# A fourth dense tile by accumulating DMAs, and the last tile's lists made inside the expert sweep

## What is computed

```python
def peer(h, w_pq, sub_keys, u_tab, v_tab):
    q = (hf @ w_pq).reshape(T, PEER_HEADS, 2, PEER_HALF)          # 8 heads, 2 halves of 128
    s = jnp.einsum('thsd,hskd->thsk', q, sub_keys)                # 128 sub-keys per half
    s_top, i_top = lax.top_k(s, PEER_TOPK)                        # 16 best per half: "lists"
    cand_s = (s_top[:, :, 0, :, None] + s_top[:, :, 1, None, :])  # 16 x 16 candidates
    f_s, f_pos = lax.top_k(cand_s, PEER_TOPK)                     # 16 pairs per head
    ids = jnp.take_along_axis(cand_i, f_pos, axis=-1)             # "decode": 128 ids per token
    g = jax.nn.softmax(f_s)
    u = jnp.take(u_tab, eb, axis=0)
    a = jax.nn.gelu(jnp.einsum('tkd,td->tk', u, xb), approximate=False)
    return jnp.einsum('tk,tkd->td', wb * a, jnp.take(v_tab, eb, axis=0))
```

## Time and profile before

| | us |
|---|---|
| median of 3 runs | 3486.44 (3481.64 to 3489.65) |
| the profiled execution | 3488.68 |
| its span, first to last instruction | 3486.9 |
| of it: inputs of the mixer | about 340 |
| middle stage, to its end at | 1168.2 |
| one-hot stage (weigh), to its end at | 1318.7 |
| two sweeps and what follows | the rest |
| PE busy | 3315.8 (95%) |
| DVE busy | 2639.6 (76%) |
| POOL busy | 1314.3 (38%) |
| ACT busy | 1274.5 (37%) |

### The profile page before, as it was taken

The page is one execution under the profiler, slowest core; times in us unless marked ns, Lnnn a source line. Parts: engine busy times, 40 slices in busy tenths (PEclk is TensorE's granted clock), DMA queues, the critical chain, the costliest instruction groups (busy, mean ns, idle before and its releaser), DMA issues.

```text
span 3486.9 us, 46941 instructions
## 1 busy us (share of the span) xinstructions
PE 3315.8 (95%) x17312; PEld 2792.9 (80%) x17312; DVE 2639.6 (76%) x5361; ACT 1274.5 (37%) x2402; POOL 1314.3 (38%) x824
## 2 busy tenths in 40 slices
PE   8999999999998477999999999999999999999997
PEld 3656367787887467999999999998999999999996
DVE  0223127888888996888888888889899998888866
ACT  1232133343332593333333333333434333333333
POOL 1000000788886005777775232322233333232201
PEclk9999999999998898999999999999999999999998
DMA  9300544666666149999999999998998999999943
GB/s 397 137 20 8 229 163 164 196 169 180 178 178 190 73 193 349 353 353 348 347 346 364 354 358 355 375 354 332 368 356 347 373 363 354 360 349 360 352 163 124
DMA packets 270605, 952.87 MB, mean 273 GB/s; under 512 B 74281, under 2 KB 127657, under 8 KB 211121
## 3 DMA queue, kind: packets, MB, share of 16 engines
q1 hardware_dynamic: 154898, 521.75, 40.4%
q0 software_dynamic: 115200, 428.07, 34.6%
q10 hardware_dynamic: 288, 0.16, 0.0%
HBM read 888.70 MB, written 61.18 MB: 272 GB/s over the span
## 4 chain that ended last, share of the span: by engine, by line
PE 60%; DVE 1%; DMA 0%; ACT 0%; issue 0%; SPq 0%; DVEq 0%; ACTq 0%
PE bank L1561 30%; PE bank L1575 30%; DMA uw<-in_u 0%; DVE slots L1692 0%; DMA vw<-x_scratch 0%; DVE uL L1756 0%; DVE ring L1668 0%; DVE st L1716 0%; DVE slots L1713 0%; DVE slots L1731 0%; DVE hL L1660 0%; DVE slots L1734 0%; DVE vL L1751 0%; ACT hR L1609 0%; DVE accS L1685 0%
## 5 line engine op out<-in xcount | busy, mean ns | idle before, releaser
L1524 POOL DMA_INDIRECT ring<-in_uv,slots x384 | 587.7, 1530 | 1217.4 <-DVE accS L1685 976.1
L143 POOL DMA_INDIRECT g_cells<-slots x384 | 670.7, 1747 | 381.5 <-DVE slots L1217 248.1
L1561 PE MATMUL bank<-hR,uR 128*128 128x384 f32 x2048 | 689.0, 336 | 18.2 <-DVE uL L1756 18.2
L1561 PE MATMUL bank<-hR,uL 128*128 128x384 f32 x2048 | 688.9, 336 | 0.0
L1561 PE MATMUL bank<-hL,uR 128*128 128x384 f32 x2048 | 687.6, 336 | 0.0
L1685 DVE SCALAR_TENSOR_TENSOR accS<-ring,cs,accS 128x1024 f32<-128x1024 f32 x381 | 489.5, 1285 | 13.6
L1575 PE MATMUL bank<-vR,cR 128*128 128x512 f32 x1536 | 477.5, 392 | 0.7 <-DVE slots L1692 0.7
L1575 PE MATMUL bank<-vR,cL 128*128 128x512 f32 x1536 | 476.0, 391 | 0.0
L1575 PE MATMUL bank<-vL,cR 128*128 128x512 f32 x1536 | 475.7, 391 | 0.0
L1622 ACT ACTIVATE cR<-ga 128x384 fp32r<-128x384 f32 x256 | 134.6, 526 | 927.8 <-PE bank L1575 831.2
L1668 DVE CUSTOM_DVE_ANT_0 ring<-ring,slots 128x1024 f32<-128x1024 f32 x384 | 467.0, 1253 | 0.0
(11 more groups left out here) (240 smaller groups left out, 4007.1 us busy)
## 6 DMA issues: line engine op xcount, KB each, us to landing
uw<-in_u SPq DMA_DIRECT2D x256, 512.0 KB, 6.2
vw<-in_v SPq DMA_DIRECT2D x256, 512.0 KB, 7.3
wr<-in_w_pq SPq DMA_DIRECT2D x36, 2048.0 KB
wr<-in_w_o SPq DMA_DIRECT2D x18, 2048.0 KB
g_cells<-free POOLq DMA_DIRECT2D x32, 768.0 KB, 7.1
g_blocks<-stage SPq DMA_DIRECT2D x12, 2048.0 KB, 6.3
gw<-g_blocks SPq DMA_DIRECT2D x32, 768.0 KB, 14.0
gw<-g_cells SPq DMA_DIRECT2D x32, 768.0 KB, 9.6
```

Source lines behind the costliest of these rows:

```text
L143: pool.indirect_dma_start(out=g_dram[1][:, :], out_offset=bass.IndirectOffsetOnAxis(ap=slots[:, i, D + k:D + k + 1].bitcast(U32), axis=0), ...
L1524: pool.indirect_dma_start(out=ring[:, k % R, :], out_offset=None, in_=a["uv"], in_offset=bass.IndirectOffsetOnAxis(ap=ids[:, k // P, k % P ...
L1561: mm = pe.matmul(A[t][:, 0:CW], w[:, t, k, :], h[:, k, :], start=(k == 0 and w is uR and h is hR), stop=(k == DK - 1 and w is uL))
```

## The change

Three things, which need each other.

1. **Tile 3 moves from one-hot to DMAs.** DMA_TILES = (3, 0, 1, 2) get their g by indirect DMAs, so POOL issues 512 of them instead of 384; tile 3's go to g_blocks, whose four blocks for it are stored with zeros before (16 more DMAs in mixer_inputs). Only tiles 4 and 5 (ONE_HOT) are left in weigh. GROUPS is now a list written out; 16 groups run in the middle stage, three in weigh (LATE = 19), and 13 in the sweep, which at two DMAs per step fill its first 104 steps. In decode tile 3's cell numbers take five small operations on DVE (token, cell0). SP waits for tile 3's last group before the first load of gw.
2. **Tile 8's lists and decode leave the middle stage.** Its scores are left in a new tile, carry (which lies outside the stages' own memory and also serves as xt, hT, s, and two of the three accumulators). DVE makes the lists and the decode in sixteen pieces (PIECES) in the sweep's steps 1, 6, ... 76, between uL and ga; ACT makes two spreads and one exponential there. The gathers of tile 8 wait for routed. In the middle stage residual_in of tile 8 moves ahead of the lists of tile 7.
3. **The buffer of v is two deep for the first 84 steps** (VBUF), since the third part of vw holds the pieces' small tiles; from step 84 it is three again.

```diff
 EARLY = 16
+LATE = 19
+DMA_TILES = (3, 0, 1, 2)
+ONE_HOT = (4, 5)
-GROUPS = wavefront()
+GROUPS = list(in_turn((1, 1, 2, 1, 2, 3, 2, 3, 0, 0, 1, 0, 0, 2, 0, 0, 3, 0, 0, 1,
+                       3, 2, 1, 3, 2, 1, 3, 2, 1, 3, 2, 3)))
...
 def place(pool, slots, g_dram, placed, d, h, first=0, last=TOPK):
-    i = DENSE[1][d]
+    i = DMA_TILES[d]
...
+                for b in range(P // TB):
+                    for part in range(4):
+                        pool.wait_ge(zeroed[part], (NZ // 4 + b) * 16)
+                        ks = slice(part * NKEY // 4, (part + 1) * NKEY // 4)
+                        pool.dma_start(g_dram[0][ZB + b, :, ks, :].rearrange("p k t -> p (k t)"),
+                                       zero[:, 0:NKEY // 4 * TB]).then_inc(zeroed[part], 16)
...
-                    if n > 2 * H:
+                    if 0 <= n - 2 * H - 1 < LAST * H:
                         spread(*divmod(n - 2 * H - 1, H))
...
-                spread(NT - 1, H - 1)
-                exps(NT - 1)
...
                     if h == 0 and i >= 3:
                         decode(i - 3)
-                    if 0 <= i - 2 < NT:
+                    if h == 0 and i - 1 == LAST:
+                        residual_in(LAST)
+                    if 0 <= i - 2 < LAST:
                         lists(i - 2, h)
-                    if h == 0 and 0 <= i - 1 < NT:
+                    if h == 0 and 0 <= i - 1 < LAST:
                         residual_in(i - 1)
-                decode(NT - 1)
...
-        DT = DENSE[0]
+        DT = ONE_HOT
...
                 pool.iota(iob[:, :], pattern=[[1, P]], base=0, channel_multiplier=0,
                           allow_small_or_imprecise_dtypes=True).then_inc(const, 1)
+                for d, h in GROUPS[EARLY:LATE]:
+                    place(pool, slots, g_dram, placed, d, h)
...
+    VBUF = [g % 2 if g < 84 else g % 3 for g in range(GT)]
+    VUSE = [VBUF[:g].count(VBUF[g]) for g in range(GT)]
+    PIECES = {1 + 5 * x: divmod(x, 3) for x in range(3 * H + 4)}
...
-                    if g >= VB:
-                        sp.wait_ge(v_l, g - VB + 1)
-                    sp.dma_start(vw[:, g % VB, :], a["v"][g % NEt, :, :]).then_inc(v_in[g % VB], 16)
+                    b = VBUF[g]
+                    if VUSE[g]:
+                        sp.wait_ge(v_l, max(x for x in range(g) if VBUF[x] == b) + 1)
+                    elif b == 2:
+                        sp.wait_ge(routed, NT)
+                    sp.dma_start(vw[:, b, :], a["v"][g % NEt, :, :]).then_inc(v_in[b], 16)
...
                         if n == 0:
+                            if m == 0:
+                                sp.wait_ge(placed[0], PAIRS * 16)
                             sp.dma_start(gw[:, b % 2, :].rearrange("p (c w) -> p c w", c=CB),
...
+                    if g in PIECES:
+                        part, piece = PIECES[g]
+                        if part < H:
+                            (best_8, next_8, pairs)[piece](part)
+                        elif part == H:
+                            (compare, select_0, select_1)[piece]()
+                        else:
+                            store()
```

More of the change, by code:

```diff
@@ L55 @@
 DENSE = ((3, 4, 5), (0, 1, 2))
+LAST = NT - 1
 NS = len(STILES)
@@ L61, with in_turn @@
 EARLY = 16
+LATE = 19
 RATE = 2
-def wavefront():
-    place = {(d, h): 4 * d + 2 * h for d in range(CT) for h in range(PH)}
-    return sorted(place, key=lambda dh: (place[dh], dh[0]))
-GROUPS = wavefront()
+DMA_TILES = (3, 0, 1, 2)
+ONE_HOT = (4, 5)
+ZB = DENSE[0].index(DMA_TILES[0]) * P // TB
+def in_turn(order):
+    seen = {d: 0 for d in order}
+    for d in order:
+        yield d, seen[d]
+        seen[d] += 1
+GROUPS = list(in_turn((1, 1, 2, 1, 2, 3, 2, 3, 0, 0, 1, 0, 0, 2, 0, 0, 3, 0, 0, 1,
+                       3, 2, 1, 3, 2, 1, 3, 2, 1, 3, 2, 3)))
 class Count:
@@ L1490, in _ @@
                             if m == 0:
-                                for d in range(CT):
+                                for d in range(1, 1 + CT):
                                     sp.wait_ge(placed[d], PAIRS * 16)
@@ L1523, in gather @@
                         pool.wait_ge(v_done, k - R + 1)
+                    if k == STILES.index(LAST) * P:
+                        pool.wait_ge(routed, NT)
                     pool.indirect_dma_start(
@@ L1642, in _ @@
                         act.activation(ga[:, x % 2, :], A[x % 2][:, 0:CW], ACT.Gelu).then_inc(a_ev, 1)
+                    if g - 1 in PIECES:
+                        part, piece = PIECES[g - 1]
+                        if (part, piece) == (1, 1):
+                            spread(0)
+                        if (part, piece) == (H, 0):
+                            exps()
+                        if (part, piece) == (H, 1):
+                            spread(1)
                     if g in NSTEP:
@@ new lines, in next_8 @@
+                def next_8(g):
+                    sl4 = range(4 * g, 4 * g + 4)
+                    for l in sl4:
+                        ins = dve.max(top[:, l, 8:TOPK], s[:, l, :])
+                    ch.step(ins)
+                    for l in sl4:
+                        ins = dve.max_index(ti[:, l, 8:TOPK], top[:, l, 8:TOPK], s[:, l, :])
+                    ins.then_inc(listed, 1)
+                    dve.wait_ge(listed, H * LAST + g + 1)
+                    dve.tensor_copy(itb[:, 4 * g:4 * g + 4, :], ti[:, 4 * g:4 * g + 4, :]).then_inc(key_in, 1)
+                    pair = top[:, 4 * g:4 * g + 4, :].rearrange("p (h w) k -> p h w k", w=2)
+                    dve.tensor_tensor(
+                        cand[:, :, 0:PAIRS].rearrange("p h (a b) -> p h a b", b=TOPK),
+                        pair[:, :, 0, 0:8].rearrange("p h (a o) -> p h a o", o=1).to_broadcast([P, 2, 8, TOPK]),
+                        pair[:, :, 1, :].rearrange("p h (o b) -> p h o b", o=1).to_broadcast([P, 2, 8, TOPK]),
+                        ALU.add)
+                    ch.step(dve.tensor_tensor(cand[:, :, PAIRS:CAND], pair[:, :, 0, 8:TOPK],
+                                              pair[:, :, 1, 0:1].to_broadcast([P, 2, 8]), ALU.add))
@@ new lines, in pairs @@
+                def pairs(g):
+                    for half in range(2):
+                        sl = slice(half * 8, half * 8 + 8)
+                        for h in range(2):
+                            ins = dve.max(fs[:, 2 * g + h, sl], cand[:, h, :])
+                        ch.step(ins)
+                        for h in range(2):
+                            ins = dve.max_index(fp[:, 2 * g + h, sl], fs[:, 2 * g + h, sl], cand[:, h, :])
+                        ch.step(ins)
+                        if half == 0:
+                            for h in range(2):
+                                ins = dve.match_replace(cand[:, h, :], fs[:, 2 * g + h, sl], cand[:, h, :], LOW)
+                            ch.step(ins)
@@ new lines, in select, with select_0 @@
+                def select(half):
+                    part = eq[:, 8 * half:8 * half + 8, :, :]
+                    dve.wait_ge(key_out, H * LAST + half + 1)
+                    dve.tensor_tensor(part, part, key[:, :, :, :], ALU.mult).then_inc(decoded, 1)
+                    dve.wait_ge(decoded, LAST + half + 1)
+                    for n in (8, 4, 2):
+                        ch.step(dve.tensor_tensor(part[:, :, 0:n, :], part[:, :, 0:n, :], part[:, :, n:2 * n, :], ALU.add))
+                def select_0():
+                    select(0)
@@ new lines, in select_1, with store @@
+                def select_1():
+                    select(1)
+                def store():
+                    for w in range(2):
+                        ins = dve.tensor_tensor(out[:, w, :].rearrange("p (h s) -> p h s", h=PH),
+                                                eqw[:, :, w, 0, :], eqw[:, :, w, 1, :], ALU.add)
+                    ch.step(ins)
+                    dve.scalar_tensor_tensor(slots[:, LAST, D:D + PAIRS].bitcast(U32), out[:, 0, :], float(NKEY),
+                                             out[:, 1, :], ALU.mult, ALU.add)
+                    dve.wait_ge(e_out, NT)
+                    ch.step(dve.tensor_reduce(hm[:, :], fs[:, :, :], axis=AX.X, op=ALU.add))
+                    ch.step(dve.reciprocal(hi[:, :], hm[:, :]))
+                    dve.tensor_tensor(
+                        slots[:, LAST, D + PAIRS:].rearrange("p (h k) -> p h k", h=PH), fs[:, :, :],
+                        hi[:, :].rearrange("p (h o) -> p h o", o=1).to_broadcast([P, PH, TOPK]),
+                        ALU.mult).then_inc(routed, 1)
+                    dve.wait_ge(routed, NT)
```

145 lines of the change are left out of this document (114 added, 31 removed).

## The result

| | before | after | second profile of after |
|---|---|---|---|
| median (lowest to highest) | 3485.61 (3481.64 to 3489.65), 4 runs | 3436.53 (3427.03 to 3444.26), 4 runs | 3436.42 (3428.08 to 3438.68), 5 runs |
| span of the profiled execution | 3486.9 | 3424.9 | 3436.5 |
| POOL's first scatter at | 611.67 | 608.26 | 609.78 |
| from there to the end of the middle stage | 556.7 | 528.4 | 535.3 |
| one-hot stage | 150.5 | 121.5 | 122.0 |

What follows compares the result with a forecast made beforehand. TensorE was taken to bound the sweep, but not the middle stage's end or the one-hot stage. Terms -27 - 29 + 1.5 + 1 = -53.5 us turn the profiled 3488.7 into 3435.2, median 3433; range 3408 to 3458.

Steps and rivals of the forecast that it cites:

- The likeliest case: Whole kernel: the forecast itself, all terms summing to -53.5 us, so 3433; chance 0.56.
- POOL ends the middle stage: Rival, middle stage: landing gaps or scatters meeting decode push POOL's 16 groups past 1141, to 1150; kernel 3442; chance 0.1.
- End of the middle stage, -27: Middle stage without tile 8's lists and decode ends at 1141 instead of 1168.2: 27 us won, bounds 33 and 18.
- 1128, or 1140 with gaps of 5.9: Middle stage: time in us when POOL finishes its 16 groups, with landing gaps of 2.5 or of 5.9.
- The four neighbours' waits: Middle stage: four places where two groups of one tile follow each other on POOL, 2.5 us of landing each.
- still ahead of 1141, just: Middle stage: POOL, done by 1128 or 1140, ends before the stage's new end at 1141.
- The one-hot stage, -29: One-hot stage: one scatter per 2.74 us while DVE works; POOL ends it after about 121.5 us, 29 us won.
- The rival in which a scatter does not wait: Rival, one-hot stage: scatters do not wait for DVE, whose 102.8 us set the stage; kernel 3414; chance 0.15.
- Start of the sweep, +1.5: Start of the sweep: SyncE waits for tile 3's last scatter before loading g's weights; 1.5 us lost, bounds 0 and 6.
- The sweep, +1: Sweep: pieces hidden in DVE's spare time, scatters and two v buffers nearly free; 1 us lost, bounds 0 and 25.
- The rival of a stretched sweep: Rival, sweep: two v buffers, u behind g and 40 more scatter steps cost 25 us; kernel 3458; chance 0.14.
- The zero stores: First stage: 16 more zero stores go out while POOL has nothing else to do; no cost.

Runs made afterwards that it cites:

- second profile of after: The changed kernel as it is, nothing altered, run and profiled once more: 3436.42 us.
- a later run: Changed kernel with scatters reordered in the middle stage, two groups in the one-hot stage, tile 8's residual_in behind tile 7's lists: 3428.26 us.
- the version without the wait: Changed kernel with all three edits, plus three scatters of tile 2 between tile 3's two groups in the one-hot stage: 3401.84 us.
- the first experiment: Changed kernel with two groups instead of three in the one-hot stage, tile 2's group moved to the sweep: 3424.83 us.

## Why the prediction was right

**The time.** 3433 was forecast and 3436.5 measured. The likeliest case came true in the first profile of the changed kernel; in the second the rival "POOL ends the middle stage" did, in a smaller size (535.3 us from the first scatter, where 1150 - 611.7 is 538). That the median lies as close as 3.5 us is in part luck: which engine ends the middle stage, with ends 7 us apart, is decided by about 1 us between a scatter and a load, and the working had nothing of that.

**End of the middle stage, -27.** -28.3 in the first profile, -21.4 in the second; the bounds were -33 and -18. PE and ACT end at 528.4 from the first scatter where 1141 - 611.7 = 529.3 was forecast, and the shift of DVE is real: 5.98 us of wait, 5.9 us of stage (522.5 against 528.4, both with POOL out of the way). What the working left out is that ACT also holds tile 8's sd (1073.68) behind the spread of tile 7, so the norm waits for the lists too. POOL was the weak step. "1128, or 1140 with gaps of 5.9" is 516 to 528 us after the first scatter; it was 521.8 and 530.2. (With its own numbers, 611.7 + 16 x 30.9 + 11.7 + 4 x 5.9 is 1141.4, so level with the 1141 and not ahead of it.) The four neighbours' waits were 2.55, 7.83, 4.40 and 2.51 or 10.96 where 2.5 each stood (the trace of the kernel before had both sizes with their surroundings: ahead of its 5.90 SP issued a load of wr 3.4 us before the end of the scatter waited for, at 670.3 us, and around its 2.44 none within 6 us), and the step "still ahead of 1141, just" had no term for the 5.1 us between POOL's last scatter and the end of the stage. With it, POOL and PE are level, and one landing decides.

**The one-hot stage, -29.** -29.0, 121.5 us as forecast. The 2.74 us lock is in every profile with tensor_tensors; DVE's path alone is seen in the 102.0 to 102.4 of the versions with fewer scatters there (102.8 forecast; DVE ends 9.5 us ahead of that and SP issues the last store 6.4 us ahead). Two small errors cancel: the last scatter was out 117.3 us into the stage and not 121.5, since the first ones ran beside an idle DVE and the landing took 1.68; and 4.2 us of stage change came on top, which the sum did not have. The rival in which a scatter does not wait is refuted here. So is, for these scatters, the inference of the Trainium skill ("SBUF — State Buffer", "Who interferes with whom") that a tensor_tensor leaves descriptor generation alone; its rule ahead of that, that a DVE instruction with two SBUF inputs contends with a GpSimd one that reads SBUF, agrees with 2.44 us beside tensor_tensors and 1.69 on average beside copies. What no term held is the 45.68 us of a later run.

**Start of the sweep, +1.5.** 0. SP's load of gw follows its first load of u after 0.39 us, as in before: the 4.2 us until the stage ended already contained the landing.

**The sweep, +1.** -1.3 and +1.4 in the two profiles, so nothing that can be told. The pieces take 1.6 to 4.1 us (2.6 to 4 forecast; only the last one is under 2.6). That DVE's spare time hides them is shown by the pieces in a row (+32 us) and only partly by the sum over five steps (+7 when moved to steps with a pair). The two buffers for v cost nothing, with or without the third behind step 84. The rival of a stretched sweep did not appear at its size with 104 steps of scatters, nor with 112. Its mechanism did: ACT waits for a late u, up to 5.5 us, on five to seventeen steps in every profile of these kernels, nearly always behind a load of g, and the slack of about 4 us that the prediction gave PE hides most of it. With the pieces in their own places it cost PE one wait of 1.2 to 2.4 us in four of the profiles and less than 0.4 us in the others.

**The zero stores.** From 120 to 140 us the DMA engines are now at 0.88 where they were at 0.00, and PE is busy 17.85 us of it against 17.75, 16.96 in the second profile, where the first scatter is still 1.9 us earlier than before: nothing that can be told, as forecast.

## What to carry to other kernels

When work moves onto an engine with room, add what its end costs the stage and compare the two engines within that margin: two chains within 5 us of one another make a kernel whose runs differ, and one profile shows only one side. Put independent work between accumulating DMAs that must wait for each other's landing: here that took POOL off the end of the middle stage, 7 us against the second profile, and in the one-hot stage the hold of 45.68 us was not seen again, in one profile and by the times of five runs (3400 to 3410). Beside a DVE that runs tensor_tensors without a pause, a scatter costs its own 1.54 us and the time to the end of the DVE operation that it meets, here 2.44 us in all, so that one scatter goes out per unit of 2.74.

## What the runs showed of the hardware that was not expected

- A scatter can be held for 45.68 us, through sixteen units of DVE operations with two SBUF inputs that run without a gap. It was seen once in thirteen profiles, after a landing wait of 5.24 us; starts at seven other places of the unit did not bring it about. The seven waits of 1.6 to 1.8 us beside tensor_tensors were each followed by an ordinary scatter; the three other waits of over 5 us ended in DVE's last unit or behind it, so no other profile tries a long wait with DVE still at work. That the same hold explains all five slow runs with that order (3425 to 3436, where the version without the wait has 3400 to 3410) and the 26 us between the runs of the first experiment fits, but only the profiled run shows it. What holds it stays open.
- The landing of a small indirect DMA is seen after 1.6 to 3.0 us when the last 2 MB transfer was issued 8 us or more ahead of the scatter's end; after 9.1 to 11.0 when one was issued 0.7 to 1.0 us ahead of that end; after 5.2 to 8.0 with one 1.6 to 3.4 us ahead, and after 4.2 to 6.2 with one 4.9 to 6.5 us ahead. A transfer issued behind the end didn't show.
- A stage that ends on POOL's indirect DMAs ends 4.2 us (one-hot, 3.1 once) or 5.1 us (middle) after the last of them; the middle stage that ends on ACT's work ends 0.3 us after it, and the one-hot stage that ends on a store 6.4 us after that was issued.
